# Sample attention of a hybrid decoder step: states loaded from GpSimd's queue at the prompt mixers' end, a ring of three key and value buffers, the output weight earlier, and two output tiles between the attention steps

## The reference, cut to what matters

```python
def dilated_attention_sample(q, kc, vc):        # kc, vc: 2048 cached keys/values + 8 new ones
    for window, dil in ((128, 1), (512, 4), (2048, 16)):
        idx = W + ti[:, None] - dil * j[None, :]
        s = einsum('bthd,btjhd->bthj', q, kc[:, idx])
        ...
    return combine_by_denominator(outs, lses)

# mLSTM of one sequence's chunk, with states C, n, m that come in and go out
num = w_inter * einsum('bhtd,bhde->bhte', qc, C) + einsum('bhts,bhse->bhte', sc, vc)
C_new = wT_inter * C + einsum('bhs,bhsd,bhse->bhde', wT, kc, vc)

mix = concat([attention, mlstm])
x = x + einsum('btc,cd->btd', mix, w_out)       # then x + MLP(RMSNorm(x)), and a last RMSNorm
```

## Time and profile before

| | |
|---|---|
| median of 3 runs | 2770.88 us (2768.64 to 2771.23) |
| the profiled execution, its own time | 2770.26 us |
| its span, first to last instruction | 2768.4 us |
| PE busy | 2615.6 us (94% of the span) |
| DVE, ACT, POOL busy | 1780.3, 1045.1, 685.4 us |
| moved by DMA | 620.08 MB, mean 224 GB/s |

### The profile page before, as it was taken

The page is one execution under the profiler, slowest core; times in us unless marked ns, Lnnn a source line. Parts: engine busy times, 40 slices in busy tenths (PEclk is TensorE's granted clock), DMA queues, the critical chain, the costliest instruction groups (busy, mean ns, idle before and its releaser), DMA issues. The chain is left out here.

```text
span 2768.4 us, 44506 instructions
## 1 busy us (share of the span) xinstructions
PE 2615.6 (94%) x16803; PEld 2209.4 (80%) x16803; DVE 1780.3 (64%) x3800; ACT 1045.1 (38%) x1927; POOL 685.4 (25%) x585
## 2 busy tenths in 40 slices
PE   7999999999899996779989999899999999999997
PEld 6888788878777784558867888799998888778886
DVE  6722566332688884467667766765555677887778
ACT  4312333010566773123355555555553112221113
POOL 1167212120255453121210000100002333333232
PEclk9999999999999998889999999999999999999999
DMA  4367543264455547967846877778859777887672
GB/s 186 140 213 271 192 149 128 96 207 142 131 173 160 157 160 261 373 249 274 309 139 228 273 266 266 263 256 302 299 199 351 271 252 243 274 300 237 217 263 88
DMA packets 341548, 620.08 MB, mean 224 GB/s; under 512 B 38303, under 2 KB 241187, under 8 KB 327638
## 3 DMA queue, kind: packets, MB, share of 16 engines
q1 hardware_dynamic: 271980, 521.85, 54.5%
q10 hardware_dynamic: 68218, 91.38, 9.2%
q0 software_dynamic: 1152, 4.19, 0.4%
HBM read 446.84 MB, written 237.61 MB: 247 GB/s over the span
## 5 line engine op out<-in xcount | busy, mean ns | idle before, releaser
L3551 DVE TENSOR_TENSOR mlp_acc<-mlp_acc,bank 128x512 f32<-128x512 f32 x440 | 298.5, 684 | 141.4 <-PE bank L2839 135.7
L2837 PE MATMUL bank<-mlp_wd,mlp_u_hi 128*128 128x512 f32 x896 | 350.4, 391 | 8.8 <-DVE mlp_acc L3551 5.1
L2838 PE MATMUL bank<-mlp_wd,mlp_u_hi 128*128 128x512 f32 x896 | 349.2, 390 | 0.0
L2839 PE MATMUL bank<-mlp_wd,mlp_u_lo 128*128 128x512 f32 x896 | 349.2, 390 | 0.0
L3320 ACT ACTIVATE mlp_u_hi<-mlp_u_raw 128x768 fp32r<-128x768 f32 x126 | 113.1, 946 | 446.6 <-POOL mlp_u_raw L3188 446.2
L2837 PE MATMUL bank<-mlp_h_hi,mlp_wu_hi 128*128 128x272 f32 x896 | 259.2, 289 | 9.3 <-DVE mlp_h_lo L3409 4.8
L2838 PE MATMUL bank<-mlp_h_lo,mlp_wu_hi 128*128 128x272 f32 x896 | 258.8, 289 | 0.0
L2839 PE MATMUL bank<-mlp_h_hi,mlp_wu_lo 128*128 128x272 f32 x896 | 258.0, 288 | 0.0
L292 PE MATMUL p_bank<-p_w_hi,p_hT_hi 128*128 128x512 f32 x640 | 250.4, 391 | 7.8 <-DVE p_stage L836 7.8
L294 PE MATMUL p_bank<-p_w_hi,p_hT_lo 128*128 128x512 f32 x640 | 249.1, 389 | 0.0
L293 PE MATMUL p_bank<-p_w_lo,p_hT_hi 128*128 128x512 f32 x640 | 249.1, 389 | 0.0
(11 more groups left out here) (444 smaller groups left out, 5935.4 us busy)
## 6 DMA issues: line engine op xcount, KB each, us to landing
mlp_wd<-wd SPq DMA_DIRECT2D x31, 2048.0 KB, 8.3
mlp_wd<-wd SPq DMA_DIRECT2D x32, 1536.0 KB, 7.4
mlp_u_raw<-u SPq DMA_DIRECT2D x256, 128.0 KB, 2.4
out_win_k_sample<-in_cache_k SPq DMA_DIRECT2D x48, 680.0 KB, 8.2
out_win_v_sample<-in_cache_v SPq DMA_DIRECT2D x48, 680.0 KB, 8.9
mlp_wu_raw<-in_w_up SPq DMA_DIRECT2D x31, 1024.0 KB, 6.2
p_w_raw<-in_w_tok SPq DMA_DIRECT2D x10, 2048.0 KB
wd<-mlp_un_hi SPq DMA_DIRECT2D x21, 896.0 KB, 4.4
```

What stands on the lines that cost most here:

```text
L2837: nc.tensor.matmul(out, ah, bh, start=fresh and k == 0, stop=False, skip_group_check=not fresh)
L2838: nc.tensor.matmul(out, ah, bl, start=False, stop=False, skip_group_check=not fresh)
L2839: ins = nc.tensor.matmul(out, al, bh, start=False, stop=k == n - 1, skip_group_check=not fresh)
L3551: v.tensor_tensor(a, a, b[:], ALU.add).then_inc(summed, 1)
```

## The change

- *The mixers' end.* V0 is loaded by SP at the end of `mix_prompt`, behind the second keys, into a place of its own. POOL issues the loads of the states C there, behind its product `hg` (L1474) of the last chunk and ahead of `hb` (L1490).
- *The ring.* `k_first`, V0 and C get places of their own. A class `Ring` lays the other keys and values into three homes in the order K1, K2, V1, V2, K4, V3, K5, V4, K6, V5, K7, V6, V7; K3 goes where the first keys lay. Each load waits for the use of the piece three loads earlier.
- *SP's list* sends new values, K2 and V1 at once, K3 after the first scores, and only then waits for the mixers' stores. The output weight, two tiles of partial results, the gain and x of tiles 0 and 1 go out between K4 and V5. ACT's wait for the mixers' stores moves from its beginning to b = 5, POOL gets one ahead of its masked keys.
- *The order on PE.* The state products come after the first half of b = 1, ahead of the second half of 0; the state updates move to the first halves of 2 and 3. Tile 0 is turned after the first half of 6, its products stand behind the second half of 5 and behind the first half of 7, where tile 1 is turned too; tile 1's products and the turn of tile 2 stand between the turn of the last probabilities and their value products.
- *DVE and ACT* follow: `rest` of quarters 2 and 3 and the blend of tile 0 after the second half of 4, the blend of tile 1 after that of 5, the additions of x for tiles 0 and 1 within the stage. The blend works in place. POOL makes its quarters 1 and 0 of the weight after the mLSTM's result.
- `project_out` starts with the products of tile 2 (`EARLY = 2`), makes `norm_turn(0)` after its first half, and no longer loads the gain. The space for descriptors of POOL's transfers is set to 8192 bytes.

```diff
@@ mix_prompt, SP and POOL
                     load_keys(sp, K.k_second, K.ins["cache_kt"], 1, K.k_second_in)
                     K.small.load_rows(K, sp)
+                    load_window(sp, K.v_first, K.ins["cache_v"], 0, K.v_first_in)
...
                     g_.tensor_tensor(hg[:].rearrange("p h d -> p (h d)"), hh[:].rearrange("p h d -> p (h d)"), gs[:],
                                      ALU.mult).then_inc(s["hg"], 1)
+                    if m + 1 == NCH:
+                        pool.wait_ge(s["scores"], T.count)
+                        for h in range(MH):
+                            pool.dma_start(K.Cs[:].rearrange("p (b h) c -> p b h c", h=MH)[:, :, h, 0:MD],
+                                           K.ins["state_C"][:, h].rearrange("b d e -> d b e")).then_inc(K.C_in, 16)
@@ mix_sample, SP
-            for b in range(DEC_B - 1):
-                if b + 2 < DEC_B:
-                    sp.wait_ge(s["scores"], 4 * b + 3)
-                    load_k(b + 2)
...
+            def used(kind, b):
+                if kind == "k":
+                    sp.wait_ge(s["scores"], 4 * b + 3)
+                else:
+                    sp.wait_ge(s["summed"], b + 1)
...
             sp.dma_start(vnew[:], K.proj[VK, S0:S0 + NS, :]).then_inc(s["vnew_in"], 16)
+            load("k", 2)
+            load("v", 1)
+            load("k", 3)
+            mixers_stored(sp)
...
+            load("v", 2)
+            load("k", 4)
+            load("v", 3)
+            sp.wait_ge(s["hb_ready"], 1)
...
+            used("v", 0)
+            O.load_w(sp, 1)
+            O.load_w(sp, 2)
+            load("k", 5)
+            sp.wait_ge(s["fin"], 16 * 3)
+            O.load_w(sp, 0)
+            sp.wait_ge(s["C_out"], 16 * MH)
+            O.load_w(sp, 3)
+            O.load(sp, 0)
+            load("v", 4)
+            sp.dma_start(K.to_mlp.gain2[:], K.ins["norm2_g"].partition_broadcast(P)).then_inc(O.gain_in, 16)
+            sp.wait_ge(s["turned"], T.turned("p", 3, 3))
+            O.load_x(sp, 0)
+            load("k", 6)
+            sp.wait_ge(K.state_out, 16)
+            O.load(sp, 1)
+            load("v", 5)
+            O.load_x(sp, 1)
+            load("k", 7)
+            load("v", 6)
+            load("v", 7)
@@ mix_sample, PE
             first_half(1)
-            second_half(0)
-            first_half(2)
             pe.wait_ge(s["act_ml"], 3)
             pe.wait_ge(s["pool_own"], 6)
             pe.wait_ge(s["C_in"], 16 * MH)
...
+            second_half(0)
+            pe.wait_ge(s["own"], 3)
+            first_half(2, 0)
             second_half(1)
-            pe.wait_ge(s["own"], 3)
-            first_half(3, 0)
-            second_half(2)
-            first_half(4, 6)
+            first_half(3, 6)
...
+            second_half(2)
+            first_half(4)
+            second_half(3)
+            first_half(5)
+            second_half(4)
+            first_half(6)
+            turn(0)
+            second_half(5)
+            products(0, 0)
+            first_half(7)
+            products(0, 1)
+            turn(1)
+            second_half(6)
+
+            def last_tiles():
+                products(1, 0)
+                products(1, 1)
+                turn(2)
+
+            second_half(7, last_tiles)
@@ project_out, PE
-            for t in range(1, NP + 1):
+            for t in range(O.EARLY, NP + 1):
                 products(t, 0)
+                for n in range(O.EARLY - 1) if t == O.EARLY else ():
+                    norm_turn(n)
                 if t + 1 <= NP:
                     turn(t + 1)
                 products(t, 1)
```

More of the change, by code:

```diff
@@ L1835, in products_first, with products @@
-    def products_first(self, pe, e, bank, part):
-        cols = slice(512 * e, 512 * e + 512)
+    def products(self, pe, t, e, out):
+        cols, p = slice(512 * e, 512 * e + 512), t % 2
         def split(k):
-            if e == 0 and k % 2 == 0:
+            if t == e == 0 and k % 2 == 0:
                 pe.wait_ge(self.w_lo_ready[k // 2], 1)
         if e == 0:
[L1843 to L1846, removed]
+            pe.wait_ge(self.lo_ready, t + 1)
+        if t:
+            pe.wait_ge(self.added, 2 * t + e - 1)
+        split_products(self.K.nc, out, [(self.mT_hi[:, p, k], self.mT_lo[:, p, k], self.w_hi[:, k, cols], self.w_lo[:, k, cols])
+                                        for k in range(KC)], self.prod_mm, split)
@@ L1848, in round, with add @@
+    def add(self, dve, t, e, out):
+        x = self.xt[t % 3]
+        if e == 0:
+            dve.wait_ge(self.x_in[t % 3], 16 * (t // 3) + 16)
+        dve.wait_ge(self.prod_mm, 2 * t + e + 1)
+        self.K.nc.vector.tensor_tensor(x[:, 512 * e:512 * e + 512], x[:, 512 * e:512 * e + 512], out, ALU.add).then_inc(self.added, 1)
     def round(self, act, q):
@@ L1947 @@
 KEYS = OLD + NS
-HOME = 12
 QW = 32
@@ L2006, in turned @@
     def turned(self, kind, b, i):
-        return self.place[kind, b, i] + 1
+        return self.count[kind, b, i]
     def out(self, kind, b, i):
@@ L2014, in free, with __init__, home, before @@
         return self.copied[n] if n >= 0 else None
+class Ring:
+    HOMES = 3
+    def __init__(self):
+        order = [("k", 1), ("k", 2), ("v", 1), ("v", 2)]
+        for b in range(4, DEC_B):
+            order += [("k", b), ("v", b - 1)]
+        order.append(("v", DEC_B - 1))
+        self.order = order
+        self.place = {g: n for n, g in enumerate(order)}
+        self.landing, counts = {("k", 3): 16}, [0] * self.HOMES
+        for n, (kind, b) in enumerate(order):
+            counts[n % self.HOMES] += 16 if kind == "k" else 32
+            self.landing[kind, b] = counts[n % self.HOMES]
+    def home(self, kind, b):
+        return self.HOMES if (kind, b) == ("k", 3) else self.place[kind, b] % self.HOMES
+    def before(self, kind, b):
+        if (kind, b) == ("k", 3):
+            return "k", 0
+        n = self.place[kind, b] - self.HOMES
+        return self.order[n] if n >= 0 else None
 SAMPLE_ROWS = 5
@@ L2112, in mix_sample, with homes, home @@
-        qz = front("qz", DEC_B, PAIRS, QW)
-        pT = front("pT", HOME + 1, P)
-        mask, mask_new = sb("mask", [P, OLD]), sb("mask_new", [P, DEC_B, NS])
-        osb = sb("osb", [P, DEC_B, 2 * HD])
-        st = sb("st", [P, 2, 8])
+        R = Ring()
+        def homes(at, end):
+            used = [at]
+            def home(name, *shape):
+                here, used[0] = used[0], used[0] + -(-int(np.prod(shape[1:])) // 8) * 8
+                assert used[0] <= end, name
+                return K.place("sm_" + name, here, list(shape))
+            return home
@@ new lines, in mix_sample, with kin, vin @@
+        ring = [(K.place(f"sm_ring_k{n}", at, [P, PAIRS, OLD]), K.place(f"sm_ring_v{n}", at, [P, WT, AW]))
+                for n, at in enumerate((B_AT, A_AT, C_AT, K0_AT))]
+        assert B_AT + WT * AW <= A_AT and A_AT + WT * AW <= SMALL_AT and C_AT + WT * AW <= GAIN_AT
+        def kin(b):
+            return ring[R.home("k", b)][0] if b > 1 else (K.k_first, K.k_second)[b]
+        def vin(b):
+            return ring[R.home("v", b)][1] if b else K.v_first
+        home = homes(SMALL_AT, C_AT)
@@ L2225, in _ @@
             assert own.n == 6
-            pool.wait_ge(s["scores"], 3)
-            for h in range(MH):
-                pool.dma_start(by_head[:, :, h, 0:MD], K.ins["state_C"][:, h].rearrange("b d e -> d b e")).then_inc(s["C_in"], 16)
+            mixers_stored(pool)
             pool.wait_ge(s["own"], 1)
@@ L2238, in _ @@
                 pool.dma_start(K.o["C_sample"][0, :, h].rearrange("b d e -> d b e"), by_head[:, :, h, 0:MD]).then_inc(s["C_out"], 16)
-            pool.wait_ge(s["scores"], 4 * 6 + 3)
-            for q in range(2):
+            pool.wait_ge(s["hb_ready"], 1)
+            for q in (1, 0):
                 pool.wait_ge(O.w_in[q], 16)
```

343 lines of the change are left out of this document (160 added, 183 removed).

## The result

The changed kernel takes 2778.2 us (median of 7 executions, 2772.9 to 2782.8); the kernel before, timed beside it, 2770.0. The ratio is 1.0028, 95% interval 1.0016 to 1.0040: slower, by little, but by more than the 0.2% named in the prediction. 2759 had been forecast, and the range ended at 2771. The profiled execution of after took 2773.8 us, so it is one of its quicker ones.

A forecast was written before the change was run, and what follows sets the result against it. TensorE was taken to bound the kernel nearly everywhere, except the sample attention, where the DMA engines are full. Gains of 3.9 us there and 7.3 in the output projection, 11.2 together, took 2770.26 to 2759; range 2741 to 2771.

The forecast's parts named there:

- Part 1: Start of the sample attention's stream: 4.7 MB of early values and states close the first DMA hole.
- The states: At the state products: states land near 1090, so PE waits 0 to 4 us, not 14.5.
- what the early transfers pass: At the mixers' end: POOL's queue is passed by nothing that hurries; its four issues take 3.7 us.
- has that time: At the mixers' end: the last stores lie behind 2.62 MB on SP, but POOL, SP and ACT can wait.
- Part 2 and 3: Sample attention's ring and end: next stage starts near 1221.8, not 1225.66, so 3.9 us won.
- Part 4: Output projection: tile 2's 12.0 and an old wait of 1.3 go, a new wait of 6 comes; 7.3 us won.
- V5 that ends last: Stage's end: V5 lands near 1178; from then PE's own work of 43.7 us ends last.
- these hidden until V5 lands: Stage's end: sequence 6's masks, queued on DVE behind two weight subtractions and a blend, stay hidden if done by V5's landing.
- The two stops of the stream: Middle of the stage: 4 us lost as K4 waits for scores, 3 as SP waits for the mLSTM's result.
- C: Sample attention: storing the new states blocks SP's queue; 2765 to 2766, or 2768 if 8 us or more late; chance 0.16.
- E: Mixers' end: waits hold SP and POOL, so the loads aren't early; 2763 to 2770; chance 0.03.
- D: Sample attention: states land late, 2770, or 2780 if POOL's issues also block and delay the barrier; chance 0.12.

The follow-up runs named there:

- arg_sp: Changed kernel with ScalarE's five small loads issued by SyncE instead, ahead of sample 1's keys; 2771.6 us, ratio to before 1.0003.
- out_first: Changed kernel with tile 2's input rows and tile 4's parts asked for ahead of the sample's eight stores in the output projection; 2771.4 us, ratio 0.9994.
- best1: Changed kernel, values early; gate arguments and masks on SyncE before sample 1's keys, two weight pieces earlier, tile 4 before the sample's stores; 2759.9 us, ratio 0.9958.
- best2: Changed kernel with sample 0's values at the old place, gate arguments on SyncE's queue, tile 4's parts ahead of the sample's stores; 2760.4 us, ratio 0.9966.
- best3: Changed kernel with values at the old place, gate arguments and masks early on SyncE, two weight pieces earlier, tile 4 before the sample's stores; 2758.6 us, ratio 0.9953.
- mask_early: Changed kernel, values still early, with gate arguments and both mask tables on SyncE's queue ahead of sample 1's keys; 2766.3 us, ratio 0.9988.

## Why the prediction was wrong, point by point

**Part 1 fell, and with it the sum.** The states: right, in time, no stand at their products. The step that failed is the sentence on what the early transfers pass: it went through the queues of SyncE and GpSimd, and named the stores and GpSimd's next work. It did not ask what other queues would send into the same DMA engines in that stretch. ScalarE's five small loads were in the trace of before (2.75 and 1.22 us, at 1066 to 1070), beside 75 to 214 GB/s: cheap because of the very hole that was to be filled. Price: 9.3 to 9.9 us at the barrier, in all four profiles of the unmended early transfers, and behind it mask tables that land 5 to 19 us after their issue. The passage also says that whoever waits for the mixers' stores "has that time". SyncE's last store now lands late: in arg_sp GpSimd waits 9.8 us for it, though in after the barrier hides that.

**Part 2 and 3, the stage: 3.9 forecast, 6.2 measured.** Of this, 17.1 us were won up to sample 1's value products (1084.9 to 1119.2, that is 34.4, where before took 51.5, from 1072.3 to 1123.9) and 11.0 given back behind them, mostly the second tile, which the sum books in part 4. The end came out close: 42.7 us from sample 5's value products to the projection (43.7 forecast). But it isn't V5 that ends last there: it was in at 1184.6 (issued at 1163.3, landed 21.3 us later; 1178 forecast), and its products start at 1189.3 with no wait for it. TensorE waits for K5 (7.8), V4 (7.1) and K6 (3.9), and then 3.7 for the masks of sequence 6, which stand behind two subtractions of the weight and a blend on VectorE; the prediction had these hidden until V5 lands. The two stops of the stream were there (0.63 in 1110 to 1120, SyncE at the mLSTM's result until 1131.9). One sum of part 2 is 0.2 us off (its terms give 1110.9, not 1110.7); nothing hangs on that.

**Part 4: 7.3 forecast, 2.6 measured.** The mechanism was right, a wait of tile 3 on tile 4's loads; what the sum lacked is a stand for ScalarE and the clock's two falls. Tile 3's first product came 23.7 us after the stage's start, not 21.2 (15.2 + 6). TensorE's stands up to there add up to 6.3, near the 6 that were booked, but the first of them isn't tile 4's:

```profile
1242.57 0.63 PE L2870 MATMUL bank<-ident,out_ma 128*128 128x128 f32 x4 [2.37 <-ACT out_hs L2729]
```

It waits for ScalarE's copy of the first norm turn, which the sum doesn't have; 0.70 and 3.21 follow. Behind the 2.37 the granted clock is 0.62 in 1242.5 to 1247, between its two levels, and behind the 3.21 it is 0.50 in 1255.7 to 1260.5 (0.63 us for each product, 0.39 later). The first of these falls makes most of the 2.2 that are left of the 23.7: from tile 3's turn to the next norm turn it takes 8.1 us, one tile later 6.3. The second took another 2.2: from tile 3's first product to the next stage it is 185.6 us against 183.4 before. With the loads put first, the 3.21 are gone and the 2.37 stay; the projection is then 202.6 in out_first and 202.7 in best1, best2 and best3, below even the 204.6 of the forecast (211.9 - 7.3).

**The rivals.** C didn't come: the weight's last piece was asked for at 1141 without a stand. Nor did E: SyncE asked for the first values at 1060.9 and GpSimd for the states at 1062.6. D gave the right band (2770 to 2780), the right direction and the sign to look for, "a barrier later than 1072", but by a cause that wasn't there: the states weren't late, and GpSimd's issues took 3.70 us as before. The chance for it, 0.12, covered a mechanism on the wrong engine. The rule that a VectorE instruction with two SBUF inputs and a GpSimd one that reads SBUF exclude each other (the Trainium skill, "SBUF — State Buffer", "Who interferes with whom") found its rows in the projection, beside GpSimd's multiplication by the gain, 4.09 against 1.90 us; in after VectorE stood 5.69 us behind them, so these 2.2 us were not on the path. Beside GpSimd's two subtractions, at 1146.7 and 1157.7, VectorE's work for the attention took no longer than elsewhere (0.42 to 0.69 us), as the prediction assumed.

What stays open: in which executions the mask lands late, and how much of the 8.2 us between the medians that makes. The same code gave 4.6, 5.1, 5.8 and 17.8 us for the first table, and 5.1, 5.7, 11.2 and 19.0 for the second. That mask_early, with all these small loads ahead, lies 11.0 below the changed kernel speaks for the small loads as the whole of it, but no trace counts the cases. The spread of the times doesn't tell: 9.9 us over 7 executions of the changed kernel, but 12.0 over 12 of mask_early, where the masks are early.

## What to carry to other kernels

A hole in the DMA engines' share is not free room: before filling it, list every transfer that any engine issues in or just behind it, and ask who stands at a barrier for it. A transfer that nobody needs soon (here the values) is worth nothing early, and must go behind the small ones that somebody needs at once. A new wait in a queue can be mended by order alone: 6.7 us of the projection for a few lines on SyncE's list.

## What the runs showed of the hardware

That the issue of a load can block its engine was not expected from a trace where it took 0.7 us. The same four loads of 16 KB took 2.75, 7.22, 8.22 and 12.81 us of ScalarE's time, with 2.6, 5.2, 4.7 and 7.3 MB of keys, values and states asked for on other queues in the 12 us before them. It isn't ScalarE's queue alone: SyncE's 128 KB of new values took 8.3, 10.7 and 10.5 us to issue in arg_sp, mask_early and best1, and 0.46 in after. What is issued into full engines can also land late: SyncE's last store of the mixers' results (256 KB), issued at 1073.1 in after, took 12.6 us to land, 3.3 in before. The share of the DMA engines was 0.98 to 1.07 in these stretches, but what they moved fell to 331 to 334 GB/s in 1075 to 1085, against 396 to 412 in the earlier trace rows at a like share. Small packets have a part in that: ScalarE's queue takes 9.1% of the engines' time in 1055 to 1100 with the 0.08 MB of small loads and 5.1% without them, so by these shares they cost an estimated 1.8 us of all 16 engines. Why the issue itself waits, no run here shows.

The Trainium skill ("DMA: Bandwidth & Descriptors", "Issuing engines are not separate DMA queues") says that transfers run on the same 16 engines whichever engine issued them, and that the time to issue one "is usually small relative to the DMA itself". The runs agree with the first half: the states on GpSimd's queue and the values on SyncE's delay ScalarE's loads alike. On the second this case is an exception, and the measurement decides: 12.81 us to issue 64 KB, in an engine that a barrier waits for.
